# Down projection in seven block products over six chunk pairs instead of four, with weight sums made by accumulating DMAs

## The chip, the cores and the metric

One core of a Trainium2 chip runs the whole program. The metric is the device time of one execution in microseconds (us), lower is better.

## The reference, cut to what matters

Two kinds of transformer block, two layers each, on x of 256 tokens by 1024, all in float32. Every layer has two feed-forward parts (eight in all) around a mixing part, which the change leaves alone:

```python
def swiglu(h, w1, w3, w2):            # h 256x1024, w1 and w3 1024x2816, w2 2816x1024
    return (jax.nn.silu(h @ w1) * (h @ w3)) @ w2
h = rmsnorm(x, g_ffn1[l])
x = x + 0.5 * swiglu(h, w1_a[l], w3_a[l], w2_a[l])
```

## The kernel before, in words

**Precision.** Every float32 operand is split in two float32r parts, hi (ACT rounds it) and lo (DVE subtracts). A product is hi*hi + hi*lo + lo*hi, so three matmuls.

**Units.** Weights come as numbered units of up to 128x2048 (1 MB). SP loads a unit into one of `RAW` = 3 slots of `raw` in two DMAs (`load`, L464); ACT writes its hi part (`split`, L1290, counted by `hi_done`); DVE its lo part (L1788, counted by `w_ready`); both parts lie in one of `HL` = 4 slots of `split_w`. PE multiplies and counts `w_used`. A load waits until the ring unit three places before it is split by DVE; an ACT split waits until the unit four numbers before it is used by PE. The order of instructions on each engine is written out by hand, and each engine runs its own list in order.

**Gate/up phase.** 22 blocks of 128 hidden columns (`FC` = 22), one unit each. PE (`hidden_chunks`) does 16 matmuls of 512 and 16 of 256 columns. ACT copies the low half of the bank (`low_parts`, L1367), DVE adds (L1932, twice), scales the gate (L1937), ACT applies silu (L1373), DVE multiplies (`hidden`, L1942), ACT rounds (L1378), DVE subtracts (`hidden_lo`, L1948). All these are 128x256 instructions, one set for every block.

**Down phase.** The 22 chunks of 128 rows of w2 times two column halves of 512. Fourteen chunks (`ALONE`) are multiplied plainly: 2 halves x 2 token halves x 3 matmuls of 512 columns each. The other eight form four pairs. The 2x2 blocks of a pair (two chunks by two column halves, named 11, 12, 21, 22) are multiplied with seven block products (Strassen's way, Winograd's form) instead of eight: `U`, `T2`, `T4`, `T3` with sums of weight blocks, `11`, `21`, `22` with blocks as they are; the sums of the left sides (`sums`, tile `sa`) are made in the gate/up phase. Each product is one unit of 2048 columns, four pairs wide. The four quarters of w2 lie whole in `early_quarters` and `late_quarters`, outside of the ring; DVE makes the four weight sums in place (`quarters_added`, L1802) and splits from there (L1795). `part_to_x` (L1978) adds finished banks to x.

`DOWN` fixes the order of the units; the waits are on `taken` (a bank was added to x) and `w_ready`. The end of a down phase feeds the next stage by transposes of x (L705) in the middle of the last units.

Of the kernel before, what the change touches and what calls it, by code (L numbers as in the profile page):

```python
# [27 lines left out]
P = 128  # L28
T = 256
# [20 lines left out]
COMBINED = ("U", "T2", "T4", "T3")  # L50
HALF_LAST = 11
# [10 lines left out]
for b in (1, 2):  # L62
    for u in (0, FFN_UNITS + MIX_UNITS[b]):
        SHORT[b].update({u + 2 * FG + i: 512 * len(part[2]) for i, part in enumerate(DOWN)
                         if part[0] == "plain" and len(part[2]) < 4})
# [3 lines left out]
FFN_RING = (True,) * (2 * FG) + tuple(part[0] == "plain" for part in DOWN)  # L69
# [125 lines left out]
def build(nc, a, known):  # L195
# [13 lines left out]
    with ctx:  # L209
        def sb(stack, name, shape, dt=F32):  # L210
# [8 lines left out]
        late_quarters = sb(late, "late_quarters", [P, 2, 2048])  # L219
# [40 lines left out]
        gate = sb(ffn, "gate", [P, 2, T])  # L260
        up = sb(ffn, "up", [P, 2, T])
# [10 lines left out]
        sa_hi = sb(ffn, "sa_hi", [P, 4, 4, P], F32R)  # L272
        sa_lo = sb(ffn, "sa_lo", [P, 4, 4, P], F32R)
        early_quarters = sb(ffn, "early_quarters", [P, 2, 2048])
        sa = sb(ffn, "sa", [P, 4, P])
        gfin = sb(ffn, "gfin", [P, D])
        ffn.close()
        quarter = {"11": early_quarters[:, 0, :], "21": early_quarters[:, 1, :],
                   "12": late_quarters[:, 0, :], "22": late_quarters[:, 1, :]}
        kept_in = {"U": "11", "T2": "11", "T4": "11", "T3": "12"}  # L280
# [116 lines left out]
        quarter_in = {q: semaphore(f"quarter_in_{q}") for q in QUARTERS}  # L397
# [26 lines left out]

        def wholes(e):
            return e.layer() + 1
# [20 lines left out]


# [4 lines left out]
        def _(eng):  # L453
# [40 lines left out]
            def quarter_load(w2, q):  # L494

                first = e.lay * FF + P * MIXED.start
                rows = w2[first:first + 4 * P * len(MIXED), :].rearrange("(k four p) n -> p k four n", four=4, p=P)
                row, col = int(q[0]) - 1, int(q[1]) - 1
                for j in range(2):
                    eng.dma_start(quarter[q][:, 1024 * j:1024 * j + 1024].rearrange("p (k n) -> p k n", k=2),  # L500
                                  rows[:, 2 * j:2 * j + 2, row, 512 * col:512 * col + 512]
                                  ).then_inc(quarter_in[q], 16)

            def alone(w2, chunks, col, u):

                k = len(chunks) // 2
                rows = [e.lay * FF + P * chunks[j * k] for j in range(2)]
                load(u, [(chunked(512 * j * k, k, 512),
                          w2[rows[j]:rows[j] + k * P, col:col + 512].rearrange("(k p) n -> p k n", p=P))
                         for j in range(2)])  # L510

            def ffn_loads(u0, f, gate_up_w, w2):
                w2 = flat(w2)
                for b in range(FC):
                    if e.unit(u0 + b) > 3:
                        gate_up(gate_up_w, e.lay * FC + b, u0 + b)
                    if b == 14:
                        eng.wait_ge(ht_done, ffn_blocks(e, f, 2))
                        quarter_load(w2, "11")
                    if b == 16:  # L520
                        quarter_load(w2, "21")
                if (e.block, e.lay) == (1, LAYERS - 1) and u0 > 0:
                    eng.wait_ge(w_used, units(e, u0, HL))
                    eng.dma_start(gfin[:, :], a["g_final"].rearrange("(a n) -> a n", a=1).partition_broadcast(P)
                                  ).then_inc(gfin_in, 16)
                for i, part in enumerate(DOWN):
                    if i == 12:
                        eng.wait_ge(w_used, units(e, u0 + 2 * FG - 1, HL))
                        quarter_load(w2, "12")
                        quarter_load(w2, "22")  # L530
                    if part[0] == "plain":
                        _, half, chunks = part
                        alone(w2, chunks, 512 * half, u0 + 2 * FG + i)
# [80 lines left out]
            for _ in e.layers(1):  # L614
                ffn_loads(0, 0, a["t_gate_up_1a"], a["w2_a"])
# [6 lines left out]
                ffn_loads(FFN_UNITS + MIX_UNITS[1], 1, a["t_gate_up_1b"], a["w2_b"])  # L622
            for _ in e.layers(2):
                ffn_loads(0, 0, a["t_gate_up_2a"], a["ffn1_w_down_2"])
# [7 lines left out]
                ffn_loads(FFN_UNITS + MIX_UNITS[2], 1, a["t_gate_up_2b"], a["ffn2_w_down_2"])  # L632
# [15 lines left out]
        def _(eng):  # L648
# [112 lines left out]
            def ffn_tensor(u0, f, next_stage):  # L761
# [77 lines left out]
                def token_half(split, c, m):  # L839
                    t = slice(m * P, (m + 1) * P)  # L840
                    return [w[:, c, t] for w in split]
# [1800 lines left out]
```

## Time and profile before

| | us |
|---|---|
| median of 3 runs (2238.1 to 2239.01) | 2238.62 |
| the profiled execution's own time | 2236.88 |
| its span, first to last instruction | 2235.1 |
| PE busy, of the span | 2228.8 |
| DVE busy | 1754.6 |
| ACT busy | 1292.0 |

The profiled execution lies 1.7 us under the median, and 1.8 us of its time lie outside of the span. PE busy counts a matmul from its start to its modelled end, and these overlap: the distance from one start to the next is what a matmul costs when PE never waits.

### The profile page before, as it was taken

How to read it: one execution, taken by the hardware profiler on the slowest of the kernel's cores; microseconds unless marked ns; L12 is line 12 of the kernel's file. 1: busy time of each engine (PE TensorE's matmuls, PEld its weight loads, DVE VectorE, ACT ScalarE, POOL GpSimd, SP SyncE). 2: the span in 40 equal slices, each digit the busy share in tenths (PEclk: the TensorE clock that was granted, in tenths of full speed). 3: DMA queues.
4: the chain of work that ended last, by engine and by line, in shares of the span. 5: the costliest groups of instructions: out<-in, count | busy, mean ns of one | idle time of the engine just before them, and what ended most of it. 6: DMA issues, size and time to landing. Idle time of an engine off the chain costs nothing.

```text
span 2235.1 us, 29208 instructions
## 1 busy us (share of the span) xinstructions
PE 2228.8 (100%) x11590; PEld 1902.8 (85%) x11590; DVE 1754.6 (79%) x2451; ACT 1292.0 (58%) x1545; POOL 0.2 (0%) x4
## 2 busy tenths in 40 slices
PE   9999999999999999999999999999999999999999
PEld 8888888888888888888888888888888888788887
DVE  7886567888788566788888799767888887976787
ACT  6655445565664544655655576565555647755663
POOL 0000000000000000000000000000000000000000
PEclk9999999999999999999999999999999999999999
DMA  7656555654565555574565553546555645355562
GB/s 266 226 180 217 166 188 182 228 197 149 201 216 171 176 171 206 170 244 142 198 222 183 190 171 127 199 163 226 179 179 202 205 156 196 105 167 195 199 216 99
DMA packets 176217, 417.64 MB, mean 187 GB/s; under 512 B 16816, under 2 KB 20784, under 8 KB 176080
## 3 DMA queue, kind: packets, MB, share of 16 engines
q1 hardware_dynamic: 175936, 415.76, 55.0%
q8 instruction: 92, 1.51, 0.3%
q14 instruction: 45, 0.37, 0.1%
q10 hardware_dynamic: 144, 0.00, 0.0%
HBM read 414.66 MB, written 1.05 MB: 186 GB/s over the span
## 4 chain that ended last, share of the span: by engine, by line
PE 93%; DVE 4%; ACT 3%; issue 1%; DMA 0%; SPq 0%; DVEq 0%; ACTq 0%
PE psum L737 25%; PE psum L673 14%; PE psum L675 14%; PE psum L674 14%; PE psum L738 13%; PE psum L867 2%; PE psum L866 2%; PE psum L864 2%; PE psum L705 2%; ACT split_w L1290 2%; DVE split_w L1788 1%; PE psum L748 1%; PE psum L1090 1%; DVE split_w L1795 0%; DVE gate L1937 0%
## 5 line engine op out<-in xcount | busy, mean ns | idle before, releaser
L1788 DVE TENSOR_TENSOR split_w<-raw,split_w 128x2048 fp32r<-128x2048 f32 (+2 forms) x373 | 807.6, 2173 | 130.5 <-ACT split_w L1290 128.7
L737 PE MATMUL psum<-xt,split_w 128*128 128x512 f32 x2464 | 859.0, 393 | 0.5 <-DVE split_w L1788 0.5
L1290 ACT ACTIVATE split_w<-raw 128x2048 fp32r<-128x2048 f32 (+2 forms) x373 | 674.9, 1821 | 128.1 <-PE psum L675 91.1
L738 PE MATMUL psum<-xt,split_w 128*128 128x256 f32 x2464 | 689.2, 280 | 0.0
L737 PEld LDWEIGHTS psum<-xt,split_w 128*128 128x128 f32 x2464 | 461.2, 187 | 104.7 <-DVE split_w L1788 2.2
L738 PEld LDWEIGHTS psum<-xt,split_w 128*128 128x128 f32 x2464 | 465.3, 189 | 0.3
L673 PE MATMUL psum<-split_w,xt 128*128 128x512 f32 (+1 forms) x736 | 289.5, 393 | 0.0
L675 PE MATMUL psum<-split_w,xt 128*128 128x512 f32 (+1 forms) x736 | 283.7, 385 | 0.0
L674 PE MATMUL psum<-split_w,xt 128*128 128x512 f32 (+1 forms) x736 | 283.6, 385 | 0.0
L673 PE MATMUL psum<-split_w,ht_hi 128*128 128x512 f32 x444 | 173.5, 391 | 0.2 <-DVE split_w L1788 0.2
L675 PE MATMUL psum<-split_w,ht_lo 128*128 128x512 f32 x444 | 172.9, 390 | 0.0
L674 PE MATMUL psum<-split_w,ht_hi 128*128 128x512 f32 x444 | 172.9, 389 | 0.0
L1373 ACT ACTIVATE gate<-gate 128x256 f32<-128x256 f32 x176 | 72.9, 418 | 158.6 <-DVE gate L1937 158.6
L673 PEld LDWEIGHTS psum<-split_w,xt 128*128 128x128 f32 x736 | 138.4, 188 | 28.9 <-issue 3.0
L675 PEld LDWEIGHTS psum<-split_w,xt 128*128 128x128 f32 x736 | 138.2, 188 | 28.0
L674 PEld LDWEIGHTS psum<-split_w,xt 128*128 128x128 f32 x736 | 138.4, 188 | 25.5
L1932 DVE TENSOR_TENSOR gate<-psum,low 128x256 f32<-128x256 f32 x176 | 74.6, 424 | 91.1 <-ACT low L1367 90.9
L1299 ACT ACTIVATE split_w<-early_quarters 128x2048 fp32r<-128x2048 f32 x40 | 76.6, 1914 | 93.6 <-DVE early_quarters L1802 76.0
L1378 ACT ACTIVATE ht_hi<-hid 128x256 fp32r<-128x256 f32 x176 | 72.7, 417 | 91.1 <-DVE hid L1942 91.1
L1367 ACT ACTIVATE low<-psum 128x512 f32<-128x512 f32 x176 | 102.2, 581 | 8.2 <-PE psum L738 6.2
L1795 DVE TENSOR_TENSOR split_w<-early_quarters,split_w 128x2048 fp32r<-128x2048 f32 x40 | 91.5, 2287 | 16.8 <-ACT split_w L1299 16.8
L1942 DVE TENSOR_TENSOR hid<-up,gate 128x256 f32<-128x256 f32 x176 | 74.1, 425 | 36.9 <-ACT gate L1373 36.0
(306 smaller groups left out, 2772.3 us busy)
## 6 DMA issues: line engine op xcount, KB each, us to landing
raw<-w_in_dram SPq DMA_DIRECT2D x180, 512.0 KB, 4.5
raw<-t_gate_up_1b_dram SPq DMA_DIRECT2D x88, 512.0 KB, 4.4
raw<-t_gate_up_2a_dram SPq DMA_DIRECT2D x88, 512.0 KB, 4.5
raw<-t_gate_up_2b_dram SPq DMA_DIRECT2D x88, 512.0 KB, 4.7
raw<-t_gate_up_1a_dram SPq DMA_DIRECT2D x84, 512.0 KB, 4.6
raw<-ffn_w_down_dram SPq DMA_DIRECT2D x48, 512.0 KB, 4.4
raw<-w_a_dram SPq DMA_DIRECT2D x24, 512.0 KB, 4.5
raw<-w_b_dram SPq DMA_DIRECT2D x24, 512.0 KB, 4.6
```

The lines of the kernel that those rows point to most:

```text
L673: nc.tensor.matmul(pair(p, m)[:, out], hi[:, c, t], whi[:, slot, w], start=first, stop=False)
L674: nc.tensor.matmul(pair(p, m)[:, out], hi[:, c, t], wlo[:, slot, w], start=False, stop=False)
L675: last = nc.tensor.matmul(pair(p, m)[:, out], lo[:, c, t], whi[:, slot, w], start=False, stop=final)
L737: nc.tensor.matmul(bank, whi[:, slot, w], xt[:, c, :, :], start=c == 0, stop=False)
L738: last = nc.tensor.matmul(bank[:, 0:T], wlo[:, slot, w], xt_hi[:, c, :], start=False, stop=c == DC - 1)
L1290: nc.scalar.activation(whi[:, e.unit(u) % HL, 0:n], raw[:, r, 0:n], ACT.Copy).then_inc(hi_done, 1)
L1299: nc.scalar.activation(whi[:, e.unit(u) % HL, :], quarter[kept_in.get(name, name)], ACT.Copy).then_inc(hi_done, 1)
L1367: nc.scalar.activation(low[:, b % 2, :, :], psum[:, first:first + 2, T:2 * T], ACT.Copy).then_inc(low_done, 1)
L1788: nc.vector.tensor_tensor(wlo[:, e.unit(u) % HL, 0:n], raw[:, r, 0:n], whi[:, e.unit(u) % HL, 0:n], ALU.subtract).then_inc(w_ready, 1)
L1795: nc.vector.tensor_tensor(wlo[:, slot, :], quarter[kept_in.get(name, name)], whi[:, slot, :], ALU.subtract).then_inc(w_ready, 1)
L1932: return nc.vector.tensor_tensor(out[:, b % 2, :], bank[:, 0:T], low[:, b % 2, j, :], ALU.add)
L1942: nc.vector.tensor_tensor(hid[:, b % 2, :], up[:, b % 2, :], gate[:, b % 2, :], ALU.mult).then_inc(hid_done, 1)
```

## The change

- `MIXED` is six pairs (chunks 2 to 13) in two groups (`SUPER` = 2) of three pairs (`PAIRS` = 3). A product is two units of 1536 columns, nine matmuls each. `ALONE` has ten chunks.
- Only `11` (of which the early sums start) and `12` (for `T3`) are loaded outside of the ring, into `early_sums` and `late_sums`. The units `11`, `21`, `22` come through the ring of three slots as the plain ones do.
- The sums `U` = 11 + 12, `T2` = U + 22, `T4` = T2 + 21 are made in `early_sums` by DMAs that GpSimd issues with `accum_op=ALU.add`, one of 768 KB for each group. Each waits until the sum before it is split. `T3` = 12 + 22 is still DVE's (`sum_added`), read from `raw`.
- w2 is laid out beforehand, so that each DMA reads one stretch a partition.
- Gate/up blocks are handled in twos: one DVE instruction adds both banks of a block (512 elements), and scale, silu, product, rounding and lo part run once for two blocks (512 elements).
- The end of the down phase has another order of `part_to_x` and splits on DVE.

```diff
-QUARTERS = ("11", "21", "12", "22")
-MIXED = range(4, 20, 4)
-ALONE = ((0, 1, 2, 3), (6, 7, 10, 11), (14, 15, 18, 19), (20, 21))
-DOWN = (("plain", 0, ALONE[0]), ("plain", 0, ALONE[1]), ("product", "11"), ("product", "21"),
-        ("plain", 0, ALONE[2]), ("product", "U"), ("product", "22"), ("plain", 1, ALONE[0]),
-        ("product", "T2"), ("plain", 0, ALONE[3]), ("product", "T4"), ("product", "T3"),
-        ("plain", 1, ALONE[1]), ("plain", 1, ALONE[2]), ("plain", 1, ALONE[3]))
+SUPER, PAIRS = 2, 3
+QUARTER = 512 * PAIRS
+MIXED = range(1, 1 + SUPER * PAIRS)
+ALONE = ((0, 1, 14, 15), (16, 17, 18, 19), (20, 21))
+DOWN = ((("plain", 0, 0),) + each("sum", "U") + each("quarter", "11") + each("quarter", "21") + (("plain", 0, 1),)
+        + each("sum", "T2") + each("quarter", "22") + (("plain", 0, 2),) + each("sum", "T3") + each("sum", "T4")
+        + tuple(("plain", 1, i) for i in range(3)))
...
+                    if b in (12, 14):
+                        s = (b - 12) // 2
+                        eng.wait_ge(ht_done, ffn_pairs(e, f, 1))
+                        sum_load(early_sums, "11", s, w2, early_in)
                 for i, part in enumerate(DOWN):
+                    if i == AT["quarter", "22", 0]:
                         eng.wait_ge(w_used, units(e, u0 + 2 * FG - 1, HL))
+                        for s in range(SUPER):
+                            sum_load(late_sums, "12", s, w2, late_in)
+                    if part[0] != "sum":
+                        down_load(u0 + 2 * FG + i, part, w2)
...
+        @block.gpsimd
+            def accumulate(q, s, w2):
+                eng.dma_start(early_sums[:, s, :], quarter(e, w2, q, s), accum_op=ALU.add).then_inc(added_in[s], 16)
+            def down_sums(u0, f, w2):
+                for s in range(SUPER):
+                    eng.wait_ge(early_in[s], 32 * (ffns(e, f) + 1))
+                    accumulate("12", s, w2)
+                for name, before in (("T2", "U"), ("T4", "T2")):
+                    for s in range(SUPER):
+                        if name in ACCUMULATE:
+                            if before in ACCUMULATE:
+                                eng.wait_ge(added_in[s], accumulated(e, f, ACCUMULATE.index(before) + 1))
+                            eng.wait_ge(w_ready, units(e, u0 + 2 * FG + AT["sum", before, s], RAW))
+                            accumulate(ADDED[name], s, w2)
...
+            def sum_added(u, f, name, s):
+                eng.wait_ge(raw_in[e.place(u) % RAW], loaded(e, u))
+                if name == "T3":
+                    eng.wait_ge(late_in[s], 32 * (ffns(e, f) + 1))
+                out = sum_tile(name, s)
+                nc.vector.tensor_tensor(out, out, raw[:, e.place(u) % RAW, 0:QUARTER], ALU.add).then_inc(combined, 1)
...
+                for i in range(1, FG):
+                    block_summed(2 * i)
+                    if 2 * i + 3 < 2 * FG:
+                        split(u0 + 2 * i + 3)
+                    else:
+                        down_split(2 * i + 3 - 2 * FG)
+                    block_summed(2 * i + 1)
+                    gate_scaled(i)
+                    if 2 * i + 4 < 2 * FG:
+                        split(u0 + 2 * i + 4)
+                    else:
+                        down_split(2 * i + 4 - 2 * FG)
+                    hidden(i)
+                    if i in MIXED:
+                        sums(i)
+                    hidden_lo(i)
+                    if i in MIXED:
+                        sums_lo(i)
...
+                splits("quarter", "11")
+                splits("quarter", "21")
+                down_split(at("plain", 0, 1))
+                used(at("quarter", "11"))
+                part_to_x(0, 0, EACH, rhalf).then_inc(taken, 1)
                 for m in range(MT):
                     part_to_x(m, 1, BOTH, rhalf)
+                splits("sum", "T2")
+                splits("quarter", "22")
+                down_split(at("plain", 0, 2))
+                used(at("sum", "T2"))
+                part_to_x(0, 1, EACH, minus_half).then_inc(taken, 1)
+                splits("sum", "T3")
+                splits("sum", "T4")
+                used(at("sum", "T3"))
+                part_to_x(1, 0, EACH, rhalf)
+                part_to_x(1, 1, EACH, minus_half)
+                used(at("plain", 0, 2))
+                part_to_x(0, 0, psum[:, 4, :], rhalf)
+                down_split(at("plain", 1, 0))
+                used(at("sum", "T4"))
+                last = part_to_x(1, 0, psum[:, 5, :], rhalf)
+                down_split(at("plain", 1, 1))
+                down_split(at("plain", 1, 2))
```

## Rows read from the trace of the kernel before

**Rows 1.** The page: span and part 1, busy us (share) and instructions.
```profile
span 2235.1 us, 29208 instructions
PE 2228.8 (100%) x11590; PEld 1902.8 (85%) x11590; DVE 1754.6 (79%) x2451; ACT 1292.0 (58%) x1545; POOL 0.2 (0%) x4
```

**Rows 2.** Busy us by stretch: PE, PEld, DVE, ACT, POOL; clock, DMA share, GB/s.
```profile
361.00:485.00 124.00, 124.00 (x716) 109.02 (x715) 100.25 (x164) 76.72 (x101) 0.00 (x0) 1.00 0.59 203
...
129.60:189.80 60.20, 58.89 (x262) 47.95 (x261) 53.17 (x42) 31.57 (x25) 0.00 (x0) 1.00 0.62 207
485.18:543.24 58.06, 58.06 (x263) 48.13 (x262) 49.71 (x38) 29.80 (x23) 0.00 (x0) 1.00 0.51 172
```

**Rows 3.** Timeline of PE, second down phase: start us, length us, instruction.
```profile
485.18 0.39 PE L673 MATMUL psum<-split_w,ht_hi 128*128 128x512 f32 x1
...
496.10 0.39 PE L864 MATMUL psum<-split_w,ht_hi 128*128 128x512 f32 x1
...
501.54 0.39 PE L673 MATMUL psum<-split_w,ht_hi 128*128 128x512 f32 x1
```

**Rows 4.** Chain of work around the first down phase: start us, us, what.
```profile
135.01 8.23 DMA late_quarters<-w_a_dram
143.33 2.30 DVE early_quarters L1802
```

**Rows 5.** Groups of DVE by form: count, busy us, mean ns of one.
```profile
L1788 DVE TENSOR_TENSOR split_w<-raw,split_w 128x2048 fp32r<-128x2048 f32 x337 | 768.0, 2287 | 117.8 <-ACT split_w L1290 116.5
...
L1788 DVE TENSOR_TENSOR split_w<-raw,split_w 128x1024 fp32r<-128x1024 f32 x24 | 29.1, 1220 | 0.3
...
L1962 DVE TENSOR_TENSOR sa_lo<-sa,sa_hi 128x512 fp32r<-128x512 f32 x32 | 22.2, 692 | 11.6 <-ACT sa_hi L1383 11.6
```

**Rows 6.** Timelines of ACT and DVE in the second down phase.
```profile
485.38 0.60 ACT L1367 ACTIVATE low<-psum 128x512 f32<-128x512 f32 x1
...
486.01 0.42 DVE L1932 TENSOR_TENSOR gate<-psum,low 128x256 f32<-128x256 f32 x1 [0.41 <-ACT low L1367]
...
504.73 2.29 DVE L1802 TENSOR_TENSOR early_quarters<-early_quarters,late_quarters 128x2048 f32<-128x2048 f32 x1
506.93 2.28 DVE L1788 TENSOR_TENSOR split_w<-raw,split_w 128x2048 fp32r<-128x2048 f32 x1
...
519.15 1.40 DVE L1978 SCALAR_TENSOR_TENSOR x<-psum,rhalf,x 128x512 f32<-128x512 f32 x2
```

**Rows 7.** Groups of ACT by form.
```profile
L1290 ACT ACTIVATE split_w<-raw 128x2048 fp32r<-128x2048 f32 x337 | 640.7, 1911 | 105.7 <-PE psum L675 79.8 <-DMA raw<-w_out_dram 11.2 <-PE psum L867 8.2
...
L1290 ACT ACTIVATE split_w<-raw 128x1024 fp32r<-128x1024 f32 x24 | 25.5, 1063 | 11.1 <-PE psum L867 10.8
L1383 ACT ACTIVATE sa_hi<-sa 128x512 fp32r<-128x512 f32 x32 | 20.3, 633 | 90.9 <-DVE sa L1957 90.9
```

**Rows 8.** Line L464, two loads each of 512 KB, then of 256 KB.
```profile
L464 SPq DMA_DIRECT2D raw<-w_b_dram x2: 368/420/471, 509.2 to 509.7; - x2
DMA to landing us min/median/max: 3.8/4.2/4.7
...
L464 SPq DMA_DIRECT2D raw<-w_b_dram x2: 340/386/433, 514.9 to 515.2; - x2
DMA to landing us min/median/max: 2.9/3.1/3.2
```

**Rows 9.** Timeline of PE at a wait in the first down phase.
```profile
156.64 0.39 PE L867 MATMUL psum<-split_w,sa_lo 128*128 128x512 f32 x1
157.22 0.50 PE L673 MATMUL psum<-split_w,ht_hi 128*128 128x512 f32 x1 [0.19 <-DVE split_w L1788]
157.56 0.39 PE L674 MATMUL psum<-split_w,ht_hi 128*128 128x512 f32 x1
```

**Rows 10.** Line L500, four loads of 512 KB of the late quarters, queued together.
```profile
L500 SPq DMA_DIRECT2D late_quarters<-w_b_dram x4: 426/466/566, 486.4 to 488.0; - x4
DMA to landing us min/median/max: 6.4/8.3/9.9
```

More of the change, by code:

```diff
@@ L218, in build @@
         late = ExitStack()
-        late_quarters = sb(late, "late_quarters", [P, 2, 2048])
+        late_sums = sb(late, "late_sums", [P, SUPER, QUARTER])
         late.close()
@@ L504, in alone, with down_load @@
[L504 to L509, printed above, removed]
+                    cols = slice(j * half, j * half + half)
+                    eng.dma_start(out[:, s, cols], quarter(e, w2, q, s)[:, cols]).then_inc(semaphore[s], 16)
+            def down_load(u, part, w2):
+                if part[0] == "plain":
+                    _, half, i = part
+                    n, rows = 512 * len(ALONE[i]), plain_rows(e, w2, half, i)
+                else:
+                    n, rows = QUARTER, quarter(e, w2, part[1], part[2])
+                load(u, [(chunked(j * n // 2, 1, n // 2), rows[:, j * n // 2:(j + 1) * n // 2].unsqueeze(1))
@@ L871, in ffn_tensor @@
-                u = u0 + 2 * FG
+                    for s in range(SUPER):
+                        u = u0 + 2 * FG + AT["quarter" if name in QUARTERS else "sum", name, s]
+                        slot = e.unit(u) % HL
+                        eng.wait_ge(w_ready, units(e, u, RAW))
+                        for k in range(PAIRS):
+                            hi, lo = LEFT[name](MIXED.start + s * PAIRS + k)
+                            w = slice(k * 512, (k + 1) * 512)
+                            final = stop and s == SUPER - 1 and k == PAIRS - 1
+                            nc.tensor.matmul(out, hi, whi[:, slot, w], start=start and s == 0 and k == 0, stop=False,
+                                             skip_group_check=resumed)
+                            nc.tensor.matmul(out, hi, wlo[:, slot, w], start=False, stop=False,
+                                             skip_group_check=resumed)
+                            last = nc.tensor.matmul(out, lo, whi[:, slot, w], start=False, stop=final,
+                                                    skip_group_check=resumed)
+                        last.then_inc(w_used, 1)
@@ L1360, in ffn_scalar @@
                 stage = f"ffn{f}"
-                second = range(MIXED.start + 1, MIXED.stop + 1, MIXED.step)
                 def low_parts(b):
@@ L1926, in ffn_vector @@
                 stage = f"ffn{f}"
-                second = range(MIXED.start + 1, MIXED.stop + 1, MIXED.step)
-                def summed(out, b, j):
-                    bank = psum[:, 2 * PAIR[b % 3] + j, :]
-                    return nc.vector.tensor_tensor(out[:, b % 2, :], bank[:, 0:T], low[:, b % 2, j, :], ALU.add)
-                def gate_scaled(b):
-                    part = gate[:, b % 2, :]
-                    nc.vector.tensor_tensor(part, part, rstd_row[:, :], ALU.mult).then_inc(scaled_done, 1)
@@ L2598, in gate_up, with down @@
         return np.stack(both, axis=4).reshape(LAYERS * FC * P, 2 * D)
+    def down(w):
+        tiles = w.reshape(LAYERS, FC, P, 2, 512)
+        pairs = tiles[:, 2 * MIXED.start:2 * MIXED.stop].reshape(LAYERS, SUPER, PAIRS, 2, P, 2, 512)
+        quarters = pairs.transpose(0, 1, 3, 5, 4, 2, 6).reshape(LAYERS * SUPER * 4 * P, QUARTER)
+        alone = tiles[:, [c for chunks in ALONE for c in chunks]].transpose(0, 3, 2, 1, 4)
+        return quarters, alone.reshape(LAYERS * 2 * P, -1)
     def gate_rows(w, bias):
```

375 lines of the change are left out of this document (175 added, 200 removed).

## Prediction

> **What bounds the kernel now.** I read the page first: PE is busy in 2228.8 of 2235.1 us, DVE in 1754.6, and POOL has nothing to do [rows 1]. Then the busy times by stretch: a gate/up phase (361 to 485) and a down phase (485.18 to 543.24) have PE busy throughout, DVE for 100.3 of 124 us and for 49.7 of 58.06, at granted clock 1.00 [rows 2]. Only the first down phase, 60.20 us long, has gaps [rows 2]. Busy PE could still be a stretched PE, so I looked at its timeline: from 496.10 to 501.54 it starts 24 matmuls of 512 columns, 0.2267 us apart, though each is shown as 0.39 long [rows 3]. So PE is at its pitch, matmuls are the only currency, and every wait that the change brings is paid in full. The second thing to see is how thin DVE's cover in the down phase is, since the change gives it another order and shorter units.
>
> **What is removed: matmuls.** A pair costs 2 chunks x 2 halves x 2 token halves x 3 = 24 matmuls plainly and 7 x 3 = 21 in seven products. Before, 14 chunks alone (168) and four pairs (84) make 252; after, 10 alone (120) and six pairs (126) make 246. Six fewer, at 0.2267 us, are 1.36 us a phase, in eight phases 10.9 us. All of that lies on PE's path.
>
> **First down phase.** It takes 60.20 us against 58.06 for the second, 2.1 more [rows 2]. The chain there goes from a load of the late quarters of 8.23 us to DVE's first sum at 143.33 [rows 4]. That sum is no longer DVE's and is made long before, so I credit 2.1 us.
>
> **Gate/up in twos.** The five 128x256 instructions of a block on DVE become, for two blocks, two sums and three others of 512 elements. A 512-element one takes 0.69 us, back to back 0.61 (below). For two blocks: 5 x 0.61 + 2 splits x 2.20 = 7.5 us, with sums of the left sides about 2 more, in the 11.0 us that PE takes for two (22 blocks in about 123). DVE had slack there and gets more. Later by one block is only `ht_done`, wanted earliest at the start of the down phase for chunks 14 and 15, which are done three pairs before. Gain 0, loss 0; PE hides it. Were this cover gone, it would cost up to 0.7 us a pair.
>
> **Durations for 1536 columns.** None is in the trace. DVE: 2.287 for 2048, 1.220 for 1024 [rows 5], so 1.755 between them; back to back 504.73 and 506.93 are 2.20 apart [rows 6], 0.085 less than the length, so 1.67. ACT: 1.911 and 1.063 [rows 7], so 1.48. An add to x: 1.40 for two [rows 6], 0.665 apart. A pair of loads of 512 KB lands 0.4 + 4.7 = 5.1 us after its first issue, a pair of 256 KB 0.4 + 3.2 = 3.6 [rows 8], so a unit of 768 KB takes about 4.35. ACT answers PE's signal after 0.2 us (485.38 after 485.18) [rows 3, 6]. After a wait, PE's first matmul takes 0.34 instead of 0.23 (157.22 to 157.56), so each wait costs 0.1 more [rows 9].
>
> **The order after, from t = 0 at PE's first matmul of the down phase.** PE, unhindered: first plain unit to 5.44; six units of nine matmuls (2.04 each: U, 11, 21) to 17.68; second plain unit to 23.1; T2, 22 to 31.3; third plain, 2.7; T3, T4.
> - DVE. ACT copies the last block from 0.20 to 0.80; DVE adds it (to 1.5), scales (2.2), splits U's second unit (3.9), multiplies (4.6), waits for ACT's rounding of 0.63 [rows 7], subtracts (5.9), splits 11's two units: ready at 7.6 and 9.3. Nothing of this can move ahead, as it starts with PE's last block.
> - The ring. 21's second unit is loaded when 11's first is split (7.6), the second plain unit when 11's second is (9.3). Before, sums and quarters went outside of the ring, and a ring slot had a whole plain unit (5.44 us) or more to refill. Now six ring units in a row have 2.04 us each. 21's second: lands at 11.9, ACT to 13.4, DVE to 15.2, wanted at 15.6; just in time.
> - The second plain unit: 9.3 + 5.1 = 14.4, behind the other load some 14.8; ACT to 16.75, DVE to 19.1; wanted at 17.68. PE waits 1.5 us. This is the step that decides most.
>
> The rows are of this very queue. The Trainium skill (DMA: Bandwidth & Descriptors, section Anatomy of one DMA) fits 2.0 us plus bytes at 436 GB/s for DMAs from GpSimd; by this the unit would take 4.4 us, the wait would be 0.8, and the sum 2241.
>
> - From there DVE has no pause: three adds to x (2.0), two splits of T2, T3's sum, split, sum, split (six times 1.67) bring 22's second unit to 31.1; PE wants it at 19.15 + 5.44 + 4.08 + 2.04 = 30.7. PE waits 0.4.
> - The end. DVE waits for T3's end (X), adds three times to x from X + 0.2, and only then splits the first unit of the second half: X + 0.2 + 2.0 + 2.29 = X + 4.5. PE has T4, 18 matmuls, 4.1 us. PE waits 0.5 (0.4 to 0.6). Before, that split stood ahead of the adds.
>
> Waits together 2.4 us, with three restarts of 0.1, 2.7 us a phase, 21.6 us in eight. Bounds: if the landing is 1 us quicker than the row, 1.7; if the queue is as slow as with four loads queued together (9.9 for the last) [rows 10], the plain unit lands 1.5 to 2 us later and it is 4.5.
>
> **The accumulating DMAs.** The trace has none. Below: like a plain load, 4.35 us for 768 KB. Above: the late quarters, 2 MB, take 1.6 + 9.9 = 11.5 us in the queue [rows 10]; three eighths of this twice over (the sum is read and written) is 8.6. I take 6, between the ends, as nothing is nearer. U's sums start in the gate/up phase, tens of us ahead. T2's start when U's units are split (-2.2 and 3.9), and must have landed by 20 and 22: hidden at either end. T4's start at 23 and 24.7 and are wanted at about 36.9 and 38.9 in the delayed course: hidden at 6 (35), not at 8.6 one after the other (40.2). They also share the DMA engines with loads; T2's second lies in 4 to 12 and touches the loads from 7.6 on, so the 1.5 is likelier too low than too high. DVE makes two sums of 1.67 us instead of four of 2.20, and splits more units with the rest. An instruction of DMA on POOL costs nobody else anything.
>
> The Trainium skill (SBUF — State Buffer, section SBUF: two separate sides) warns against just this: descriptors of a DMA from GpSimd are written through a port that VectorE can lock, and the DMA starves; by its section Who interferes with whom a tensor_tensor holds only the reading side (marked there as inferred), and this phase has little else. No row here shows either; it is a rival below.
>
> **Sum.** 2236.9 - 10.9 - 2.1 + 21.6 = 2245.5 of the profiled execution's own time; with 1.7 for the median 2247.
>
> **Rivals.** About 0.2% (4.5 us) is what a measurement of this kernel tells from no change.
> - *The ring keeps up* (other side: faster). Decided where the second plain unit lands: within 4.0 us of 9.3 PE doesn't wait there, nor behind. For it: loads in longer stretches; a landing of 3.8 for the first half of a pair. Against it: 5.1 for both [rows 8]. Then only the end's 0.6 stays: 2236.9 - 10.9 - 2.1 + 8 x 0.6 = 2228.7, median 2230. With nothing waited for, 2226.
> - *Accumulating DMAs are slow.* At 8.6 one behind the other T4's second lands at 40.2, 1.3 late; its split then holds up DVE's adds and the next split, 1.6 more. 2.9 a phase, 23 in all: 2270. It decides from 7.9 us each.
> - *Accumulating DMAs start late*, as POOL gets no turn beside a DVE that runs without pause from 19 to 33. T4's sums would start near 33 and land at 42 to 50: 3 to 11 us a phase, 2271 to 2335. For it only how full DVE is, 49.7 of 58.06 [rows 2].
> - *Gate/up in twos makes PE wait*: 0.7 us in 10 pairs x 8, 2303. Against it the slack above.
>
> **How the numbers follow.** Forecast 0.50, its own range 2238 to 2256 (waits of 1.6 to 3.8 us a phase); 0.17 of this within 4.5 us of before, 0.33 slower. Ring keeps up 0.27, all but 0.02 faster. Slow accumulation 0.15, late start 0.05, twos 0.03, all slower. Faster 0.25, same 0.19, slower 0.56. The range: 2229 leaves out a third of the ring case (0.08), 2268 half of the slow ones (0.12).
>
> **What would show it.** Right: 246 matmuls a down phase at 0.227; PE waiting at three places in each, on DVE's split of a plain unit, of 22's second unit, of the first unit of the second half; ahead of the first, ACT waiting for a DMA into `raw`; ACT not waiting for `early_sums`. Wrong: no gaps in PE in the down phase (ring case), ACT's waits on `early_sums` before T4 (slow accumulation), POOL's issues long after DVE's split (late start), PE idle in the gate/up phases. My forecast falls most easily with the landing time of one load.

## The result, and the profile after

The changed kernel takes 2256.1 us (median of 4, 2255.33 to 2258.33); the kernel before, on the same chip, 2238.36 (2237.51 to 2239.01). The ratio is 1.0081 [1.0064, 1.0099]: 0.8% slower. The forecast was 2247.0, range 2229 to 2268.

The page of the changed kernel, span and part 1, then the two large DMA queues of part 3 (packets, MB, share of 16 engines):

```profile
span 2253.5 us, 28616 instructions
PE 2226.4 (99%) x11542; PEld 1890.5 (84%) x11542; DVE 1711.6 (76%) x2067; ACT 1305.8 (58%) x1425; POOL 42.2 (2%) x52
...
q1 hardware_dynamic: 164672, 428.35, 53.8%
q0 software_dynamic: 6912, 37.75, 9.3%
```

Against [rows 1], 48 matmuls and 43 us of DVE are gone and the span is 18.4 us longer. Queue 0 is new: the 48 accumulating DMAs. Busy us by stretch, columns as in [rows 2]: a gate/up phase, the first and the second down phase.

```profile
362.00:486.00 124.00, 124.00 (x716) 108.94 (x715) 96.67 (x115) 74.17 (x82) 2.62 (x3) 1.00 0.62 206
131.03:191.36 60.33, 57.94 (x257) 46.70 (x255) 48.63 (x38) 34.62 (x27) 2.63 (x3) 1.00 0.89 282
486.73:546.60 59.87, 57.86 (x257) 46.70 (x255) 48.63 (x38) 34.59 (x27) 2.61 (x3) 1.00 0.83 259
```

The gate/up phase is as before. The second down phase is 59.87 us where it was 58.06, with six matmuls fewer and the clock at 1.00; DMA moves 259 GB/s where it moved 172. PE's gaps in that phase (start us, us):

```profile
502.19 0.39 PE L904 MATMUL psum<-split_w,ht_lo 128*128 128x512 f32 x1
502.96 0.50 PE L900 MATMUL psum<-split_w,ht_hi 128*128 128x512 f32 x1 [0.38 <-DVE split_w L1851]
...
504.92 0.40 PE L904 MATMUL psum<-split_w,ht_lo 128*128 128x512 f32 x1
506.58 0.47 PE L707 MATMUL psum<-split_w,ht_hi 128*128 128x512 f32 x1 [1.27 <-DVE split_w L1851]
...
518.02 0.39 PE L904 MATMUL psum<-split_w,sa_lo 128*128 128x512 f32 x1
518.48 0.50 PE L900 MATMUL psum<-split_w,sa_hi 128*128 128x512 f32 x1
...
531.30 0.39 PE L904 MATMUL psum<-split_w,ht_lo 128*128 128x512 f32 x1
531.98 0.50 PE L707 MATMUL psum<-split_w,ht_hi 128*128 128x512 f32 x1 [0.28 <-DVE split_w L1851]
```

I count from start to start and take 0.23 off. The waits are 0.54 ahead of 21's second unit, 1.4 ahead of the second plain unit, 0.23 ahead of 22's second, 0.45 ahead of the second half's first plain unit. (The bracketed idle counts from a matmul's modelled end, so it is less.) The same four places recur in all eight phases; only the first varies much, from 0.54 to 2.19. What stands behind the first two, by the timelines of SP, ACT and DVE, with the landing of each pair of loads:

```profile
494.34 0.88 SPq L502 DMA_DIRECT2D raw<-w_b_quarters_dram  x2
496.01 1.01 SPq L502 DMA_DIRECT2D raw<-w_b_alone_dram  x2
497.06 1.86 SPq L537 DMA_DIRECT2D late_sums<-w_b_quarters_dram  x4
```

```profile
DMA to landing us min/median/max: 4.3/4.6/4.9
...
DMA to landing us min/median/max: 4.9/5.3/5.8
```

```profile
499.62 1.49 ACT L1328 ACTIVATE split_w<-raw 128x1536 fp32r<-128x1536 f32 x1 [3.62 <-DMA raw<-w_b_quarters_dram]
502.20 1.91 ACT L1328 ACTIVATE split_w<-raw 128x2048 fp32r<-128x2048 f32 x1 [1.09 <-DMA raw<-w_b_alone_dram]
```

```profile
501.14 1.76 DVE L1851 TENSOR_TENSOR split_w<-raw,split_w 128x1536 fp32r<-128x1536 f32 x1 [3.35 <-ACT split_w L1328]
504.14 2.29 DVE L1851 TENSOR_TENSOR split_w<-raw,split_w 128x2048 fp32r<-128x2048 f32 x1 [1.24 <-ACT split_w L1328]
```

Read it as a chain. The load of 21's second unit goes at 494.34, 7.6 us into the phase as worked out, but lands at 499.6 (second half issued 494.71, 4.9 more): 5.3 us, not 4.35. ACT stood waiting for it, DVE for ACT, PE for DVE. The plain unit's load goes at 496.01, lands at 502.2, and costs the next wait. The first answers to what POOL has in flight (start us, us, and idle before, ended by DVE's split):

```profile
491.27 0.86 POOL L1817 DMA_DIRECT2D early_sums<-w_b_quarters_dram  x1 [5.46 <-DVE split_w L1858]
510.62 0.86 POOL L1817 DMA_DIRECT2D early_sums<-w_b_quarters_dram  x1 [18.49 <-DVE split_w L1858]
```

The DMA issued at 491.27 lands 6.4 us later, at 497.7, so the load ran 3.3 of its 5.3 us beside it. Over all 48 of them:

```profile
who waited for it (us, times):
  ACT split_w L1337: 4.7, 3
...
DMA to landing us min/median/max: 6.4/7.5/11.8
```

### The profile page after: what moved, and what is told of

Read it like the earlier page. It is cut to its first block, busy times and chain, and to the rows that moved or that the text cites. A ratio compares the mean times of both kernels' runs of the same rounds, so it can differ in the third digit from the quotient of the medians.

```text
span 2253.5 us, 28616 instructions
## 1 busy us (share of the span) xinstructions
PE 2226.4 (99%) x11542; PEld 1890.5 (84%) x11542; DVE 1711.6 (76%) x2067; ACT 1305.8 (58%) x1425; POOL 42.2 (2%) x52
## 3 DMA queue, kind: packets, MB, share of 16 engines
q8 instruction: 91, 1.49, 0.3%
## 4 chain that ended last, share of the span: by engine, by line
PE 87%; DVE 9%; DMA 2%; ACT 1%; issue 0%; SPq 0%; DVEq 0%; ACTq 0%
PE psum L771 25%; PE psum L772 13%; PE psum L707 12%; PE psum L709 12%; PE psum L708 12%; DVE split_w L1851 4%; PE psum L782 3%; PE psum L739 2%; PE psum L790 2%; DVE split_w L1858 1%; DVE x L2048 1%; DVE late_sums L1867 1%; PE psum L900 1%; PE psum L904 1%; PE psum L902 1%; DMA raw<-ffn_w_down_alone_dram 1%
## 5 line engine op out<-in xcount | busy, mean ns | idle before, releaser
L1851 DVE TENSOR_TENSOR split_w<-raw,split_w 128x2048 fp32r<-128x2048 f32 (+2 forms) x405 | 854.1, 2118 | 179.6 <-ACT split_w L1328 177.6
L771 PE MATMUL psum<-xt,split_w 128*128 128x512 f32 x2464 | 858.7, 393 | 0.5 <-DVE split_w L1851 0.5
L1328 ACT ACTIVATE split_w<-raw 128x2048 fp32r<-128x2048 f32 (+2 forms) x405 | 716.7, 1778 | 204.6 <-PE psum L709 95.2
L1997 DVE TENSOR_TENSOR gate_up<-psum,low 128x512 f32<-128x512 f32 x176 | 121.0, 688 | 144.1 <-ACT low L1403 144.1
L708 PEld LDWEIGHTS psum<-split_w,xt 128*128 128x128 f32 x736 | 138.4, 188 | 25.6
L707 PE MATMUL psum<-split_w,ht_hi 128*128 128x512 f32 x316 | 125.3, 397 | 13.5 <-DVE split_w L1851 13.5
L1409 ACT ACTIVATE gate_up<-gate_up 128x512 f32<-128x512 f32 x88 | 55.7, 633 | 131.5 <-DVE gate_up L2004 131.5
L709 PE MATMUL psum<-split_w,ht_lo 128*128 128x512 f32 x316 | 123.3, 390 | 0.0
L708 PE MATMUL psum<-split_w,ht_hi 128*128 128x512 f32 x316 | 123.2, 390 | 0.0
L1349 ACT ACTIVATE xt<-psum,vecs 128x256 fp32r<-128x256 f32 x88 | 34.5, 476 | 108.1 <-PE psum L739 108.1
L782 PE MATMUL psum<-xt,split_w 128*128 128x512 f32 x352 | 86.1, 393 | 1.4 <-ACT split_w L1328 1.4
L2016 DVE TENSOR_TENSOR ht_lo<-hid,ht_hi 128x512 fp32r<-128x512 f32 x88 | 60.6, 688 | 35.3 <-ACT ht_hi L1414 35.3
L707 PEld LDWEIGHTS psum<-split_w,ht_hi 128*128 128x128 f32 x316 | 59.3, 188 | 31.8 <-issue 14.5
```

Of the source, the lines that this page charges most:

```text
L707: nc.tensor.matmul(pair(p, m)[:, out], hi[:, c, t], whi[:, slot, w], start=first, stop=False)
L708: nc.tensor.matmul(pair(p, m)[:, out], hi[:, c, t], wlo[:, slot, w], start=False, stop=False)
L709: last = nc.tensor.matmul(pair(p, m)[:, out], lo[:, c, t], whi[:, slot, w], start=False, stop=final)
L771: nc.tensor.matmul(bank, whi[:, slot, w], xt[:, c, :, :], start=c == 0, stop=False)
L782: nc.tensor.matmul(pair(p, j), whi[:, e.unit(u) % HL, first:first + P], xt[:, c, :, :], start=c == 0, stop=False)
L1328: nc.scalar.activation(whi[:, e.unit(u) % HL, 0:n], raw[:, r, 0:n], ACT.Copy).then_inc(hi_done, 1)
```

## The experiments

Times are medians in us; the ratio is to the kernel before, measured on the same chip. "Waits" is from the trace of one execution: of every distance from one start to the next on PE in the eight down phases that is over 0.25 us, what lies beyond 0.227.

| kernel | time | ratio, 95% | waits |
|---|---|---|---|
| before | 2238.4 | | 3.3 |
| changed | 2256.1 | 1.0081 [1.0064, 1.0099] | 30.5 |
| twos | 2235.8 | 0.9989 [0.9979, 0.9999] | 1.3 |
| endsplit | 2251.3 | 1.0059 [1.0044, 1.0074] | 27.3 |
| noacc | 2250.6 | 1.0059 [1.0044, 1.0074] | 27.1 |
| plainearly | 2272.1 | 1.0150 [1.0135, 1.0165] | 47.3 |
| lateload | 2272.1 | 1.0159 [1.0144, 1.0174] | 46.8 |
| early_late | 2272.5 | 1.0157 [1.0140, 1.0174] | 47.9 |
| best | 2261.3 | 1.0105 [1.0090, 1.0120] | 35.7 |
| bestcopy | 2233.1 | 0.9981 [0.9972, 0.9991] | 7.6 |
| bestnoacc | 2229.2 | 0.9963 [0.9950, 0.9976] | 5.1 |
| first11 | 2243.7 | 1.0029 [1.0018, 1.0040] | 17.0 |
| spread | 2241.2 | 1.0019 [1.0010, 1.0028] | 15.7 |
| final | 2231.8 | 0.9975 [0.9966, 0.9984] | 7.2 |

The column holds more than waiting. Behind some of the longest waits the granted clock falls to its lower level, 1.2 GHz instead of 2.4, and the matmuls that follow start 0.43 us apart: 43 of them in lateload (8.6 us of its 46.8), 7 in noacc (1.4), 8 in first11 (1.6), 7 in spread (1.4), none in the other kernels. PE had waited 2.4 to 3.4 us before each fall; after waits of 2.8 and 3.5 us in two other phases of lateload and of 2.6 in endsplit it did not fall. One such place, in lateload, with its 6 us by stretch:

```profile
508.80 0.63 PE L902 MATMUL psum<-split_w,ht_hi 128*128 128x512 f32 x1
509.23 0.63 PE L904 MATMUL psum<-split_w,ht_lo 128*128 128x512 f32 x1
...
507.00:513.00 6.00, 5.50 (x16) 3.96 (x17) 4.78 (x6) 5.76 (x4) 0.00 (x0) 0.72 0.72 227
```

**twos: the kernel before with gate/up blocks in twos alone.**

```diff
-                for b in range(2, FC):
-                    gates(b)
-                    hidden_hi(b)
+                for i in range(1, FG):
+                    low_parts(2 * i)
...
+                    gates(i)
...
+                    hidden_hi(i)
```

> The kernel before with only the gate/up blocks handled in twos. My theory: PE never waits for it, 2237 to 2239.5 us; DVE busy in a gate/up phase falls by some 10 us without a gain. If the gap of 1.4 us that the changed kernel has near 23 us of its first phase comes from it, 2240. Rival, the later parts of a pair hold PE or the start of the down phase up: over 2243 us.

2235.8, a little under the 2237 to 2239.5 that I expected. The first down phase loses its gaps, 58.1 us against 60.20 in [rows 2]:

```profile
129.30:187.40 58.10, 58.10 (x267) 48.34 (x266) 49.76 (x35) 29.60 (x22) 0.00 (x0) 1.00 0.59 190
```

So gate/up in twos costs nothing, and alone it gives the 2 us that I had credited to the late quarters leaving DVE. Which of its instructions does that no run tells.

**endsplit: the second half's first split ahead of DVE's adds.**

```diff
+                down_split(at("plain", 1, 0))
                 used(at("sum", "T3"))
...
                 part_to_x(0, 0, psum[:, 4, :], rhalf)
-                down_split(at("plain", 1, 0))
```

> The changed kernel with DVE's split of the first unit of the second half put ahead of the three adds to x that wait for T3. My theory: the wait of 0.44 plus 0.11 us goes in each of the eight phases, as ACT's part is ready 0.1 us after T3; 4.4 us less, about 2251.7 us. Rival: the adds come 2.2 us later and PE waits at the transposes of x instead; 2255 to 2258 us.

2251.3: the 0.44 and its restart are gone from every phase. That term and its cause stand.

**noacc: T2's and T4's accumulating DMAs left out.**

```diff
-                for name, before in (("T2", "U"), ("T4", "T2")):
-                    for s in range(SUPER):
...
-                            accumulate(ADDED[name], s, w2)
```

> The changed kernel with the accumulating DMAs of T2 and T4 left out (their units multiply U's sum again, so this output is not the reference's); all splits, loads and matmuls stay. My theory: the waits of PE come from the ring of three slots, whose loads can only start when DVE has split 11's units; the accumulating DMA of T2 only adds about 0.9 us to the load of 21's second unit. Expected: that load lands 4.4 us after its issue instead of 5.3, PE's wait before it falls from 0.5 to 2.2 us to under 0.2, the wait before the second plain unit stays at 1.3 to 1.9, those of 0.2 and 0.44 stay; about 1 us less a phase, 2246 to 2250 us. Rival, the accumulating DMAs crowd out the loads: both waits go, 2236 to 2241 us.

2250.6, just above the 2246 to 2250 expected. The load of 21's second unit now lands 4.1 us after its issue (0.4 + 3.7, the first line below), and the wait for it is gone in seven of eight phases. Of the accumulating DMAs only T2's second was in flight beside it, so that one makes the wait in those seven.

```profile
DMA to landing us min/median/max: 3.1/3.4/3.7
...
DMA to landing us min/median/max: 3.5/4.6/5.8
```

The second line is the seventh phase, where the load still takes 6.2 us and PE still waits 1.43. So of the 8.1 us of waits at this place in the changed kernel, at most 6.7 are the accumulating DMA's. What the trace shows beside this load, and beside none of the other seven, is a transfer of 16 KB of instructions, some 0.9 us of one DMA engine; the changed kernel has it at the same point of its seventh phase, the one with the wait of 2.19. No run takes it away, so this is a guess.

PE then meets the second plain unit earlier and mostly waits 1.9 to 2.1 there: of the 9 us, 3.4 come off the waits, 4.8 without the half-clock matmuls. That load takes 6.2 us here as well, with the four late loads right behind it in the queue; no run separates these two.

**plainearly: the second plain unit right behind the first.**

```diff
-DOWN = ((("plain", 0, 0),) + each("sum", "U") + each("quarter", "11") + each("quarter", "21") + (("plain", 0, 1),)
+DOWN = ((("plain", 0, 0), ("plain", 0, 1)) + each("sum", "U") + each("quarter", "11") + each("quarter", "21")
```

> The changed kernel with the second plain unit moved up to directly behind the first. My theory: each ring unit has at least 5 us more, the waits before 21's second unit and before the second plain unit go (2.2 to 3.8 us a phase); but DVE's row of adds to x, two splits, sum, split, sum, split now starts at 19.2 and PE comes to 22's units 2 us sooner, so waits of about 0.7 and 1.3 us come up there; the 0.44 stays. Extra of PE a phase 2.4 to 3.0 instead of 3.2 to 4.7, 2246 to 2252 us. Rival, loads are slow because of the accumulating DMAs: waits on loads into raw stay wherever the units stand, 2254 to 2258 us.

A clear miss: 2272.1. The second plain unit waits no more, but the load of 21's second unit, issued 9.3 us into the phase, takes 10.2 us (in the second down phase, as all landings here unless said), PE waits 0.8 to 1.7 us for it, and three more waits of 0.7 to 1.6 follow. In flight beside it were both of T2's accumulating DMAs and the four late loads. Which of them slowed it, the next two kernels tell.

**lateload and early_late: the late loads at the start of the down phase**, in the changed kernel and in plainearly.

```diff
-                    if i == AT["quarter", "22", 0]:
+                    if i == AT["quarter", "21", 1]:
```

> The changed kernel with one thing moved: the loads of the late quarters (those of block 12) are issued ahead of the load of 21's second unit and not behind it, so that they travel in the first 8 us of a down phase, where nothing else loads, and not beside the second plain unit's load and the second accumulating DMA. Mine (the load of 21's second unit is late because bytes crowd at 6 to 18 us of the phase, its ring slot comes free where it did): its landing is hardly touched (the late loads came behind it), so the wait before 21's second unit (0.5 to 2.2 us) stays or falls by under 0.5 us, and that before the second plain unit (1.4 to 1.9 us, of which the slot is the larger part) falls by 0.3 to 1 us a phase: 2248 to 2254 us. Rival A, only the ring slot counts and not the bytes: same time, 2255 to 2257. Rival B, the early late loads push the accumulating DMAs of T2 and U back so that the sums come late: 2258 to 2262.

> The version with both plain units in front (2272.1 us) with the late loads moved ahead of the load of 21's second unit too. There that load took 10.2 us from issue to landing, with T2's two accumulating DMAs and the four late loads in flight beside it. Mine (the bytes crowd): without the late loads beside it the load lands 2 to 4 us earlier, the wait before 21's second unit (1.1 to 1.7 us) goes, T2's sums still stand behind DVE's row of adds: waits of 0.5 to 1.5 us before T2's first sum and before 22's units stay, extra down-phase waits fall from 5.3 to 6.6 us to 3 to 4.5 a phase, 2252 to 2264 us. Rival (DVE's order alone makes those waits, the load is merely slow because its issue is late): no wait goes, 2270 to 2274 us.

Both miss my theory. In early_late the late loads land by 6.8 us of the phase, ahead of the slow load, and that load still takes 9.4 us; the time doesn't move (2272.5). Their bytes were hardly what slowed it. In lateload they lie beside T2's accumulating DMAs: these land 6.9 and 8.9 us after issue, and the load of 21's second unit, issued at its old place, takes 7.5 us instead of 5.3; PE waits 2.7 to 3.5 us for it. More than half of what its waits grew by (16.3 us) is not waiting but the clock that fell behind these waits (8.6). The rival about T2's DMAs had the right sign (2258 to 2262 expected, 2272.1 measured), but what came late is the plain load, not the sums. One thing is common to both: loads beside an accumulating DMA are slow.

**best: every wait I had understood taken away at once**: both plain units first, late loads early, endsplit, and DVE's adds to x and T3's sums moved.

```diff
                 splits("quarter", "21")
+                sum_added(u0 + 2 * FG + at("quarter", "22", 0), f, "T3", 0)
                 used(at("quarter", "11"))
                 part_to_x(0, 0, EACH, rhalf).then_inc(taken, 1)
-                for m in range(MT):
-                    part_to_x(m, 1, BOTH, rhalf)
                 splits("sum", "T2")
...
                 splits("sum", "T3")
+                for m in range(MT):
+                    part_to_x(m, 1, BOTH, rhalf)
```

> The changed kernel with the four causes taken away together: the second plain unit right behind the first (its load needs no slot that the sums free), late loads ahead of the load of 21's second unit, on DVE T3's first sum ahead of 22's second split, the two x additions that wait for TensorE behind T3's splits, and the split of the second half's first plain unit ahead of the adds. Mine: all four PE waits of a down phase go or fall under 0.3 us; what is left is the six matmuls fewer a phase (8 x 1.36 = 10.9 us) and the first phase's 2.1 us: 2225 to 2232 us. Rival A, the bytes of the accumulating DMAs still crowd the loads whatever the order: one wait of 1 to 2 us a phase stays, 2234 to 2243 us. Rival B, DVE is now the limit in the first half of the down phase (its adds and splits do not fit ahead of T2): 2 to 4 us of waits a phase, 2243 to 2258 us.

2261.3, another miss, and useful as a base. The timeline of POOL there, and then two landings: of POOL's two DMAs, and of the load of 21's second unit (SP, in two halves):

```profile
492.46 0.87 POOL L1817 DMA_DIRECT2D early_sums<-w_b_quarters_dram  x1 [60.84 <-DVE split_w L1858]
496.19 0.86 POOL L1817 DMA_DIRECT2D early_sums<-w_b_quarters_dram  x1 [2.85 <-DVE split_w L1858]
```

```profile
DMA to landing us min/median/max: 6.9/8.4/10.0
...
DMA to landing us min/median/max: 8.3/8.9/9.5
```

**bestnoacc and bestcopy: the adding, and the bytes.** The first leaves out T2's and T4's DMAs, with noacc's edit; the second moves the same bytes at the same places and doesn't add.

```diff
+                if q == "12":
                     eng.dma_start(early_sums[:, s, :], quarter(e, w2, q, s), accum_op=ALU.add).then_inc(added_in[s], 16)
+                else:
+                    eng.dma_start(early_sums[:, s, :], quarter(e, w2, q, s)).then_inc(added_in[s], 16)
```

> The reordered version (2261.3 us) without the four accumulating transfers of T2 and T4 in a down phase: its T2 and T4 products read the sums as they stand, so that the output is not the reference's. There the load of 21's second unit took 9.9 us from issue to landing, beside T2's two accumulating transfers (6.9 and 10.0 us). Mine (the accumulating transfers crowd the loads beside them, and nothing else is wrong with the order): the load takes 4 to 5 us, the waits before 21's second unit (1.1 to 1.6) and T2's first unit (1.9) go, 0.3 a phase stays: 2225 to 2234 us. Rival (the order itself makes these waits: the load is issued at 9.3 us of the phase because its slot comes free then, and DVE has two additions ahead of T2): at least the 1.9 stays, 2245 to 2256 us.

> The reordered version (2261.3 us) with T2's and T4's transfers of the same size from the same queue, at the same places, but copying in place of adding, so that the output is not the reference's. It tells the bytes from the adding. If an accumulating transfer costs the rings more than its bytes (it reads and writes SBUF as well): the copies land in 3.5 to 5.5 us instead of 6.9 and 10.0, the load of 21's second unit in 5 to 7 instead of 9.9, and the time comes near that without them, 2228 to 2242 us (mine, because at 6.9 us for 768 KB alone it moves 114 GB/s where a plain load of 768 KB takes 4.1). If only the bytes count: 2255 to 2262 us.

2229.2 and 2233.1. So in this order the four DMAs a phase cost 32.1 us, of which 28.2 belong to the adding and 3.9 to the bytes. The same of bestcopy, at the same distances from the phase's start:

```profile
488.12 0.55 POOL L1820 DMA_DIRECT2D early_sums<-w_b_quarters_dram  x1 [60.35 <-DVE split_w L1861]
491.88 0.54 POOL L1820 DMA_DIRECT2D early_sums<-w_b_quarters_dram  x1 [3.21 <-DVE split_w L1861]
```

```profile
DMA to landing us min/median/max: 4.5/5.1/5.6
...
DMA to landing us min/median/max: 5.0/5.3/5.6
```

The load's second half lands 5.6 us after its issue beside copies, 9.5 beside accumulating DMAs, 3.6 beside neither (bestnoacc):

```profile
DMA to landing us min/median/max: 3.1/3.4/3.6
```

The shares of queue 0, for equal packets and bytes as the changed kernel's, say it again:

```profile
q0 software_dynamic: 6912, 37.75, 6.6%
```

and with U's alone, in bestnoacc:

```profile
q0 software_dynamic: 2304, 12.58, 3.1%
```

The page of best has 9.3% for the 6912. For the 4608 packets of T2 and T4 that is 6.2% adding (9.3 - 3.1) against 3.5% copying (6.6 - 3.1): an adding packet holds a DMA engine about 1.8 times as long. The Trainium skill (DMA: Bandwidth & Descriptors, section Issuing engines are not separate DMA queues) says that DMAs of all issuing engines run on the same 16 DMA engines and interleave; these traces agree, since SP's load is what POOL's DMA delays.

**first11: 11's units ahead of U's.** In best, the load of 21's second unit waits for 11's first split; with 11 first it goes at 4 us and not at 9.3.

```diff
-DOWN = ((("plain", 0, 0), ("plain", 0, 1)) + each("sum", "U") + each("quarter", "11") + each("quarter", "21")
+DOWN = ((("plain", 0, 0), ("plain", 0, 1)) + each("quarter", "11") + each("sum", "U") + each("quarter", "21")
```

> The reordered version (2261.3 us) with 11's units ahead of U's in all orders. The load of 21's second unit, which waits for the split of 11's first unit to free its slot, goes at about 4 us of the phase and not at 9.3, ahead of T2's accumulating transfers, which now start at about 9 and 11 us of the phase and are wanted at 20 to 22. Mine (crowded bytes, cured by spreading them): no wait before 21's second unit, under 0.7 us a phase before T2's or 22's units: 2226 to 2236 us. Rival A, the accumulating transfers now come too late, as they take 9 to 12 us beside the loads of 22: 1 to 3 us of wait a phase before T2's units, 2236 to 2252 us. Rival B, another resource than the DMA (DVE's order) holds T2: the wait of 1.9 us stays, 2240 to 2250 us.

2243.7: the load lands in 4.7 us and nobody waits for it. T2's second DMA now starts late, 15.1 us into the phase, lands 7.1 us later and PE waits 0.1 to 2.9 for it: rival A. Here a late sum does hold PE up.

**spread: U's sums back to the front, but each first unit early.**

```diff
+DOWN = ((("plain", 0, 0), ("quarter", "11", 0), ("sum", "U", 0), ("plain", 0, 1), ("sum", "U", 1), ("quarter", "11", 1))
+        + each("quarter", "21")
```

> The reordered version again, now with the first units of a down phase as first plain, 11's first, U's first, second plain, U's second, 11's second, then 21's. Against the version with 11 ahead of U (2243.7 us, which waited 0.1 to 2.9 us a phase for T2's second accumulating transfer, issued at 15 us and landed 7.1 us later, and 0.8 for 22's second unit): the two accumulating transfers of T2 go at about 4.5 and 10 us of the phase, the load of 21's second unit at about 8, 22's at 11 and 13. Mine (the accumulating transfers are long, 6.8 us and up to 10, and need to be issued 4 us ahead of where they were): no wait before T2's units, 0 to 0.3 before 22's second, down phases of 56.6 to 57.2 us: 2226 to 2233 us. Rival A (T2's transfers now travel beside the load of 21's second unit and make that late, as in the changed kernel): 0.5 to 2 us a phase before 21's second unit, 2233 to 2246 us. Rival B (DVE's row from 21's second split to 22's second, seven of 1.75 us and an addition, is the limit): 0.5 to 0.8 us a phase stays, 2232 to 2236 us.

2241.2. No rival had this wait. T2's sums are there in time, but DVE's addition ahead of T2's split stands waiting for 22's load (7.6 us from its issue to landing, beside T2's DMA), and PE waits for T2:

```profile
500.46 1.76 DVE L1854 TENSOR_TENSOR split_w<-raw,split_w 128x1536 fp32r<-128x1536 f32 x1 [3.61 <-ACT split_w L1331]
502.79 1.76 DVE L1870 TENSOR_TENSOR late_sums<-late_sums,raw 128x1536 f32<-128x1536 f32 x1 [0.57 <-DMA raw<-w_b_quarters_dram]
```

**final: those additions behind T2's splits and behind the splits of 22.**

```diff
+                    if part in (("plain", 1, 0), ("plain", 1, 1)):
+                        eng.wait_ge(combined, by_vector(e, f, "T3", part[2]))
...
-                sum_added(u0 + 2 * FG + at("quarter", "22", 0), f, "T3", 0)
                 splits("sum", "T2")
+                for s in range(SUPER):
+                    down_split(at("quarter", "22", s))
+                    sum_added(u0 + 2 * FG + at("quarter", "22", s), f, "T3", s)
```

> The order of the last version (2241.2 us) with DVE's two additions for T3 each behind the split of 22 that shares its load, and the first of them so behind T2's splits; the two loads that reuse those slots now wait for the additions. In that version T2's first unit waited 0.2 to 3.0 us a phase (7.5 us in all), because DVE's addition ahead of it stood waiting for the load of 22's first unit, which took 7.6 us beside T2's accumulating transfers. Mine: that wait goes, T2's sums landed 5 us before they are wanted and the load of 22 has 3.5 us of room, 22's second unit is ready 1.7 us earlier; down phases of 56.6 to 57.0 us but for the fourth, 2226 to 2232 us. Rival A (the accumulating transfers still push 22's load past its time in some phases): 0.5 to 1.5 us in half the phases, 2231 to 2238 us. Rival B (the two loads held for the additions are late for the second half's first plain unit): 1 to 2 us a phase there, 2236 to 2246 us.

2231.8, ratio 0.9975, within the 2226 to 2232 expected: 0.25% faster than the kernel before and 24 us under the changed one with the same operations in another order. The page, and the first and third down phases by stretch:

```profile
span 2230.0 us, 28632 instructions
PE 2220.8 (100%) x11542; PEld 1891.7 (85%) x11542; DVE 1709.1 (77%) x2067; ACT 1307.4 (59%) x1425; POOL 42.2 (2%) x52
```

```profile
131.52:188.62 57.10, 57.08 (x257) 46.86 (x255) 48.28 (x38) 34.12 (x27) 3.50 (x4) 1.00 0.93 285
...
665.33:722.45 57.12, 57.09 (x257) 46.85 (x256) 48.28 (x38) 34.20 (x27) 3.47 (x4) 1.00 0.85 261
```

Loads beside T2's DMAs are as slow as ever (22's first takes 7.8 us); they are only issued earlier than they are wanted. Of its 7.2 us of waits, 2.8 are at the start of the next stage in two phases. A ring of four slots wasn't tried.

## Why the prediction was right or wrong

- **Bound, and matmuls (-10.9).** Right: 246 matmuls a down phase at 0.227 us, clock 1.00, and every wait paid in full. The changed kernel's waits, 27.2 us more than before, less the 10.9, plus 1.5 at the start (below), make 17.8 of the 18.4 us by which the span grew.
- **First down phase (-2.1).** The old gaps went, so the size was right, but not the reason: twos removes them too, with the late quarters and DVE's sums in place.
- **Gate/up in twos (0).** Right; alone even 2 us faster. The extra 1.5 us lies in the first gate/up phase, where one of ACT's splits, at 21.28 before, waited for its load until 22.70. In the traces of the other kernels it is 0 to 2.0 us, with no pattern that I found; its cause is open.
- **Durations.** DVE 1.75 against 1.755, ACT 1.49 against 1.48; POOL's DMAs were issued within 1 us of the times worked out (second down phase: 4.5, 23.9 and 25.6 against 3.9, 23 and 24.7).
- **Second plain unit (1.5).** It measured 1.41 to 1.86, 12.6 in eight phases against 12. Right in size, partly by luck: it landed at 15.4 us instead of 14.8, and PE came 0.65 later.
- **22's second unit (0.4) and the end (0.5).** 0.21 to 0.25, and 0.44, as endsplit shows.
- **21's second unit, "just in time" (0).** This term failed. It measured 0.54 to 2.19, 8.1 us in all and 0.9 of restarts: most of the 9.1 us between 2247.0 and 2256.1. I took the load at 4.35 us from rows with no accumulating DMA beside it and had zero slack behind it. I did write that T2's second DMA touches the loads from 7.6 us on, and gave it no price. noacc shows the cause in seven phases: without it 4.1 us and no wait, with it 5.3. In the seventh phase 1.4 of the 8.1 us stay without it; their cause is open. The three terms above together give back 1.3 us, and the start adds 1.5.
- **Accumulating DMAs (6 us, 4.35 to 8.6), and the rival that they are slow.** In the second down phase three took 6.4 to 6.7, near the 6 that I took, but T4's second 11.1; median of all 7.5, at most 11.8: above my upper end. T4's two overlap, so the second lands at 36.7 us of the phase there, and not at the 40.2 of 8.6 one behind the other. ACT waited for it in three phases, 4.7 us, and PE did not. So the mechanism of that rival, a late sum, didn't act in the changed kernel; the slow DMA did its harm through the loads beside it, which none of my rivals had. In first11 a late sum did act.
- **Rival that they start late.** Refuted: POOL's instructions stand 0.5 to 0.6 us behind DVE's split in a DVE that has no pause (510.62 above, where DVE runs from 508.33 on). The starvation of which the Trainium skill warns (SBUF — State Buffer, section SBUF: two separate sides) does not show beside these tensor_tensor instructions: the DMA issued at 510.62 landed in 6.7 us.
- **Rival that the ring keeps up.** It didn't in this order; 2230 was its time, and final has 2231.8 by spreading the loads.

## What to carry to other kernels

Price a transfer not by its own landing alone but by what it does to each transfer in flight beside it, and give a load that must arrive "just in time" some room: here it came 0.5 to 2.2 us too late. An accumulating DMA takes a sum off a compute engine that may have had room for it (DVE is busy 76% here) and pays in the DMA engines; put it where nothing is awaited, and where that is impossible, issue the loads beside it earlier. In a hand-written order one late instruction holds up those behind it that are ready: mending that in spread was worth 9.4 us (2241.2 to 2231.8), after the order of the loads and sums had given 20 (2261.3 to 2241.2). And a long wait can cost more than itself, as the clock may be low behind it.

## What the runs showed of the hardware

- An accumulating DMA of 768 KB from HBM into SBUF: T2's second in the changed kernel took 6.4 to 6.9 us from issue to landing in the eight phases; T4's second, issued 1.7 us after another and with loads behind it, 9.4 to 11.8, and up to 12.3 in best. It took 0.87 us of POOL's time. Copying ones took 0.55 us of POOL's, and 5.6 and 4.5 us to land where the adding ones took 6.9 and 10.0 (T2's two, second down phase of bestcopy and best).
- A load of 768 KB in two halves: 4.0 us without such a DMA beside it, 6.0 beside two copying ones, 9.9 beside two adding ones (the same load in bestnoacc, bestcopy and best).
- TensorE's granted clock fell to half behind waits of 2.4 to 3.4 us in four kernels, and the next 4 to 13 matmuls took 0.43 us instead of 0.227; it did not fall behind every such wait.
- What the adding does inside the DMA engine no run tells. The Trainium skill (DMA: Bandwidth & Descriptors, section SDMA does more than copy) lists an addition unit in the data stream and gives no price.
